# Opening a four-layer backbone by pairs of modulation units, moving one output tile behind the long convolution, and opening the windowed layer with two query tiles

## What is computed

```
m_lat = split(silu(c)     @ mod_w[i] + mod_b[i], 6)     # shift, scale, gate | shift, scale, gate
m_ctx = split(silu(c_ctx) @ mod_w[i] + mod_b[i], 6)
u     = rmsnorm(h, g[0]) * (1 + scale) + shift          # both streams
h     = h + gate * rmsnorm(mixer(u), g[1])
u     = rmsnorm(h, g[2]) * (1 + scale') + shift'
h     = h + gate' * rmsnorm((silu(dwconv(u @ w_gate)) * (u @ w_up)) @ w_down, g[3])
# A: q,k,v = u @ w_qkv; q,k normalised and rotated; softmax(q k) v @ w_out
# B: x0,x1,v = dwconv(u @ w_in); y = longconv(v*x1) + skip*v*x1; (y*x0) @ w_out + b_out
# C: as A with a bias on q,k,v and on the output, a window of +-128, a sink logit per head
```

## Time and profile before

| | us |
|---|---|
| median of 3 runs | 2288.19 |
| profiled execution, its own time | 2291.39 |
| its span | 2289.6 |
| TensorE (PE) busy | 2175.4 (95%) |
| VectorE (DVE) busy | 1437.8 (63%) |
| ScalarE (ACT) busy | 884.0 (39%) |
| a weight tile of 1 MB, from issue to landing (median) | 5.1 |

### The profile page before, as it was taken

How to read it: one execution, slowest core, us unless ns; L and a number is a source line. 1 busy time by engine, 2 the same in 40 slices (tenths; PEclk the granted TensorE clock), 3 DMA queues, 4 the chain that set the end, 5 groups by cost and what they waited for, 6 DMA issues and landing times.

```text
span 2289.6 us, 28755 instructions
## 1 busy us (share of the span) xinstructions
PE 2175.4 (95%) x11688; PEld 1767.1 (77%) x11688; DVE 1437.8 (63%) x2212; ACT 884.0 (39%) x1329; POOL 217.5 (9%) x253
## 2 busy tenths in 40 slices
PE   5999999999999988899999999999999999998998
PEld 3877888888787756788888787478888878868996
DVE  2426558887756532667887754866787776655553
ACT  3327443332244311443332243854333223455543
POOL 0000011110010014111110001100111100100110
PEclk7999999999999999999999999999999999999999
DMA  9460335546532210334546532022454563214554
GB/s 308 141 209 19 111 101 161 171 150 217 194 126 83 83 37 19 102 100 158 166 149 220 202 103 65 1 84 82 149 165 156 184 211 120 99 45 131 185 182 140
DMA packets 224745, 304.98 MB, mean 133 GB/s; under 512 B 6738, under 2 KB 153243, under 8 KB 224486
## 3 DMA queue, kind: packets, MB, share of 16 engines
q1 hardware_dynamic: 220541, 290.11, 39.0%
q0 software_dynamic: 3664, 12.87, 1.7%
q10 hardware_dynamic: 409, 0.16, 0.0%
HBM read 302.00 MB, written 1.11 MB: 132 GB/s over the span
## 4 chain that ended last, share of the span: by engine, by line
PE 78%; DVE 10%; ACT 5%; DMA 3%; issue 2%; SPq 1%; POOL 1%; ACTq 0%; DVEq 0%; POOLq 0%
PE lo L639 16%; PE lo L640 16%; PE lo L641 16%; PE lo L705 4%; PE lo L706 4%; PE lo L707 4%; DVE w_lo L1383 2%; ACT w_hi L1059 2%; PE lo L973 2%; PE hi L705 2%; PE hi L707 2%; PE hi L706 2%; DMA w_raw<-in_ffn_w_down 1%; PE hi L986 1%; PE stat L705 1%
## 5 line engine op out<-in xcount | busy, mean ns | idle before, releaser
L639 PE MATMUL lo<-u_hi,w_hi 128*128 128x512 f32 (+1 forms) x2072 | 736.5, 355 | 9.0 <-DVE w_lo L1383 3.8
L640 PE MATMUL lo<-u_lo,w_hi 128*128 128x512 f32 (+1 forms) x2072 | 723.2, 349 | 0.0
L641 PE MATMUL lo<-u_hi,w_lo 128*128 128x512 f32 (+1 forms) x2072 | 722.6, 349 | 0.0
L1383 DVE TENSOR_TENSOR w_lo<-w_raw,w_hi 128x2048 fp32r<-128x2048 f32 (+1 forms) x182 | 406.7, 2235 | 356.9 <-ACT w_hi L1059 355.7
L1059 ACT ACTIVATE w_hi<-w_raw 128x2048 fp32r<-128x2048 f32 (+1 forms) x182 | 339.5, 1867 | 478.9 <-DMA w_raw<-in_ffn_w_down 266.7
L639 PEld LDWEIGHTS lo<-u_hi,w_hi 128*128 128x128 f32 x2072 | 394.7, 191 | 74.1 <-issue 19.3
L641 PEld LDWEIGHTS lo<-u_hi,w_lo 128*128 128x128 f32 x2072 | 394.5, 190 | 50.1
L640 PEld LDWEIGHTS lo<-u_lo,w_hi 128*128 128x128 f32 x2072 | 394.7, 190 | 49.7 <-issue 1.2
L1400 DVE SCALAR_TENSOR_TENSOR mod_acc<-mod_raw,silu_c,mod_acc 128x512 f32<-128x512 f32 x504 | 394.6, 848 | 9.9 <-DMA mod_raw<-in_mod_w 9.9
L1912 POOL TENSOR_TENSOR mid_lo<-conv,mid_hi 128x512 fp32r<-128x512 f32 (+1 forms) x88 | 117.8, 1359 | 1055.7 <-ACT mid_hi L1362 1055.7
L705 PE MATMUL lo<-w_hi,mid_hi 128*128 128x512 f32 x374 | 147.4, 394 | 3.7 <-DVE u_raw L1450 2.6
(11 more groups left out here) (296 smaller groups left out, 2698.2 us busy)
## 6 DMA issues: line engine op xcount, KB each, us to landing
w_raw<-in_ffn_w_up SPq DMA_DIRECT2D x88, 1024.0 KB, 5.1
mod_raw<-in_mod_w SPq DMA_DIRECT2D x144, 512.0 KB, 4.0
w_raw<-in_ffn_w_down SPq DMA_DIRECT2D x40, 1024.0 KB, 5.1
mod_unit<-in_mod_w SPq DMA_DIRECT2D x24, 1024.0 KB, 6.8
w_raw<-in_a_w_qkv SPq DMA_DIRECT2D x12, 1024.0 KB, 5.2
w_raw<-in_b_w_in SPq DMA_DIRECT2D x12, 1024.0 KB, 5.1
w_raw<-in_a_w_out SPq DMA_DIRECT2D x8, 1024.0 KB, 5.1
w_raw<-in_ffn_w_down SPq DMA_DIRECT2D x8, 512.0 KB, 3.6
```

Of the source, the lines that this page charges most:

```text
L639: mm(o, h3[:, k, c], x, start=(first and k == 0), stop=False)
L640: mm(o, h3[:, k, c], y, start=False, stop=False)
L641: ins = mm(o, l3[:, k, c], x, start=False, stop=(last and k == nr - 1))
L1383: tt(WL[:, n % 3, 0:words], RAW[:, n % 3, 0:words], WH[:, n % 3, 0:words].bitcast(F32), ALU.subtract).then_inc(lo_ready, 1)
```

## The change

Four parts.

1. **Opening.** The units are loaded as shift 0, scale 0, shift 1, scale 1 and so on (`UNIT_COLS`), with weight tiles 0 and 1 after units 1 and 2, and tile 2 before the rope table and units 8 to 10. A pair p of units gives shift and scale of feature chunks 2p and 2p+1. After each pair VectorE finishes those (`start_mod`), TensorE turns both streams for them (`start_turns`), ScalarE and VectorE make `u_hi` and `u_lo` (`start_his`, `start_los`), and TensorE multiplies those two chunks for tiles 0 and 1 over all 512 tokens (`start_part`). `first_tiles` is not used for layer 0.
2. **Layer B.** `fill` is gone: the last inverse stands right behind the last forward and the third inverse, and output tile 0 comes after it, at the head of `x_phase`.
3. **Layer C.** The second tile is queries 1 instead of the key tile, which becomes the third; `CH`, `TURNS` and `TURN_AT` follow.
4. **End of every sub-layer.** A Sqrt of one element stands behind the squares of the first half, so the table for Sqrt is loaded there. In the output phases of B and C `lo(L+1)` moves from block 0 to block 1, behind the diagonal.

```
-        TILES += [("c_w_qkv", _j, 0, KT, 0, TW), ("c_w_qkv", _j, 0, KT, D, P)]
-        TILES += [("c_w_qkv", _j, 0, KT, TW * t, TW) for t in range(1, 4)]
+        TILES += [("c_w_qkv", _j, 0, KT, TW * t, TW) for t in range(2)]
+        TILES += [("c_w_qkv", _j, 0, KT, D, P)]
+        TILES += [("c_w_qkv", _j, 0, KT, TW * t, TW) for t in range(2, 4)]
...
-      2: [[0, 1], [8], [2, 3], [4, 5], [6, 7], [9]],
+      2: [[0, 1], [2, 3], [8], [4, 5], [6, 7], [9]],
...
+        UNIT_COLS = [0, 4, 1, 5, 2, 6, 3, 7] + list(range(8, MB))
...
             for r in range(8):
+                if r in (2, 3):
+                    raw(r - 2)
                 unit(r)
-                if r in (3, 5):
-                    raw(r // 2 - 1)
+            raw(2)
...
             pe.wait_ge(par_ready, 2)
-            u_turns(0, 0, range(KT))
             pe.wait_ge(silu_ready, 1)
-            for r in range(8):
+            def start_unit(r):
+                if r % 2 == 0 and r > 0:
+                    pe.wait_ge(mod_final, r // 2)
                 unit_rows(r)
+            def start_turns(p, v):
+                if p == 0:
+                    pe.wait_ge(diag_ready, 2 * v + 2)
+                if 2 * p + v >= 3:
+                    pe.wait_ge(u_ready, 2 * (2 * p + v - 2))
+                for c in (2 * p, 2 * p + 1):
+                    for e in range(2):
+                        ...
+                    last.then_inc(u_turned, 1)
+            def start_part(p, n):
+                if p == 0:
+                    pe.wait_ge(lo_ready, n + 1)
+                ...
+                for k in (2 * p, 2 * p + 1):
+                    if n == 0:
+                        pe.wait_ge(*u_part(0, 1, k))
+                    for m in range(2):
+                        ... (three matmuls of 512 tokens)
+            for r in range(2):
+                start_unit(r)
                 unit_cols()
+            start_turns(0, 0)
+            start_turns(0, 1)
+            start_unit(2)
+            start_part(0, 0)
+            unit_cols()
+            start_part(0, 1)
+            for v in range(2):
+                start_unit(3 + v)
+                start_turns(1, v)
+                unit_cols()
+            start_unit(5)
+            unit_cols()
+            start_part(1, 0)
+            start_part(1, 1)
+            for v in range(2):
+                start_unit(6 + v)
+                start_turns(2, v)
+                unit_cols()
+            start_turns(3, 0)
+            start_turns(3, 1)
+            for p in (2, 3):
+                start_part(p, 0)
+                start_part(p, 1)
...
                     if w < 3:
                         forward(w + 1)
-                    else:
-                        fill()
                     inverse(w)
...
+            unit_row(0)
+            unit_row(1)
+            hi(0)
+            start_his(0, 0)
+            start_his(0, 1)
+            hi(1)
+            unit_row(2)
+            unit_row(3)
+            unit_row(4)
+            start_his(1, 0)
+            start_his(1, 1)
+            unit_row(5)
+            unit_row(6)
+            start_his(2, 0)
+            unit_row(7)
+            start_his(2, 1)
+            start_his(3, 0)
+            start_his(3, 1)
...
                 for b in range(NB):
                     o_square(k, 0, b)
+                f(R1[:, 1, 4:5], eps[:, :], ACT.Sqrt)
...
-                    if b == 0:
+                    if b == 0 and not has_bias(k):
                         lo(L + 1)
...
                         diagonal(k + 1, b)
+                    if b == 1 and has_bias(k):
+                        lo(L + 1)
...
+            start_mod(0)
             lo(0)
+            start_los(0)
             lo(1)
-            finish_mod(0, 0)
-            u_los(0, 0)
-            u_los(0, 1)
+            for p in range(1, 4):
+                start_mod(p)
+                start_los(p)
```

More of the change, by code:

```diff
@@ L273, in build @@
                             ("x1v_tok", [P, 2, 2, 512], None), ("idft", [P, 4, SEQ], None))
-        MG = [place(f"mod_unit{s}", [P, KT, TW], at=U_AT + 8 * D * s) for s in range(4)]
+        MG = [None] * 4
         MG += region(*((f"mod_unit{s}", [P, KT, TW], 8 * D * (s - 4)) for s in range(4, 8)))
@@ L311, in build @@
         uh_ready, u_ready = sem("uh_ready"), sem("u_ready")
-        group_in = [sem(f"group_in{g}") for g in range(len(MG))]
+        group_in = [None] * 4 + [sem(f"group_in{g}") for g in range(4, len(MG))]
         group_done, group_rows, group_cols = sem("group_done"), sem("group_rows"), sem("group_cols")
@@ L695, in u_turns, with x_phase @@
                     last.then_inc(u_turned, 1)
-            def x_tiles(k, X, Y, arrive, free, ts, end=False):
+            def x_phase(k, X, Y, arrive, free):
                 n0, nt, NB = XFIRST[k], XTILES[k], XN[k]
@@ L719, in finished @@
                         ins.then_inc(x_done, 1)
-                for t in ts:
+                for t in range(2 * nt - 2):
                     n, (h, tt) = n0 + t, divmod(t, nt)
@@ L752, in x_tiles @@
                 n = n0 + 2 * nt - 2
-                for b in range(NB if end else 0):
+                for b in range(NB):
                     if nt == 2:
@@ new lines, in start_part @@
+            def start_part(p, n):
+                if p == 0:
+                    pe.wait_ge(lo_ready, n + 1)
+                h3, l3 = [W[:, n, :].rearrange("p (k n) -> p k n", n=TW) for W in (WH, WL)]
+                for k in (2 * p, 2 * p + 1):
+                    if n == 0:
+                        pe.wait_ge(*u_part(0, 1, k))
+                    for m in range(2):
+                        o, c = bank[2 * n + m], slice(m * P, (m + 1) * P)
+                        mm(o, h3[:, k, c], UH[:, k, :], start=(k == 0), stop=False)
+                        mm(o, h3[:, k, c], UL[:, k, :], start=False, stop=False)
+                        last = mm(o, l3[:, k, c], UH[:, k, :], start=False, stop=(k == KT - 1))
+                if p == 3:
+                    last.then_inc(tile_done, 1)
@@ L1037, in _ @@
                     free = lambda b, i=i: ((p_evac, ahead(NH, i) + NH[i]),) if b < 2 else ((ao_lo, ahead(GROUPS, i) + GROUPS[i] - 3 + b),)
-                x_tiles(2 * i, UH, UL, arrive, free, range(KIND[i] == 1, 2), end=True)
+                x_phase(2 * i, UH, UL, arrive, free)
                 n0, q0 = FIRST["up", i], PAIR0["up", i]
@@ L1159, in _, with start_his @@
                 h_root(0, b)
-            for r in range(8):
-                unit_row(r)
-                if r in (3, 5):
-                    hi(r // 2 - 1)
-            u_his(0, 0)
-            u_his(0, 1)
+            def start_his(p, v):
+                act.wait_ge(mod_final, p + 1)
+                act.wait_ge(u_turned, 4 * p + 2 * v + 2)
+                for c in (2 * p, 2 * p + 1):
+                    f(UH[:, c, v * SEQ:(v + 1) * SEQ], start_slot(p, v)[:, (c % 2) * SEQ:(c % 2 + 1) * SEQ], ACT.Identity,
+                      scale=coef[:, v, 0, c:c + 1], bias=modv[:, v, c:c + 1]).then_inc(uh_ready, 1)
+            unit_row(0)
[16 more added lines that the diff above has]
+            start_his(3, 1)
             def exps(i, x):
@@ L1400, in mod, with start_mod, start_los, difference @@
                             stt(acc, MR[:, k % 2, j, :], S2[:, s:s + 1], acc, ALU.mult, ALU.add).then_inc(mod_step, 1)
+            def start_mod(p):
+                dve.wait_ge(group_cols, 2 * p + 2)
+                c = slice(2 * p, 2 * p + 2)
+                for v in range(2):
+                    dst, src = [x.rearrange("p (j c) -> p j c", c=KT)[:, 0:2, c] for x in
+                                (modv[:, v, :], modp[:, v * NMOD * KT:(v + 1) * NMOD * KT])]
+                    ins = tt(dst, src, col("mod_b", 0, 2 * KT).rearrange("p (j c) -> p j c", c=KT)[:, :, c], ALU.add)
+                link(ins)
+                for v in range(2):
+                    ins = stt(coef[:, v, 0, c], modv[:, v, KT + 2 * p:KT + 2 * p + 2], 1.0, col("norm_g", 2 * p, 2), ALU.add, ALU.mult)
+                ins.then_inc(mod_final, 1)
+                dve.wait_ge(mod_final, p + 1)
+            def start_los(p):
+                def difference(v, c):
+                    dve.wait_ge(uh_ready, 4 * p + 2 * v + 2)
+                    s = slice(v * SEQ, (v + 1) * SEQ)
+                    stt(ULF[:, c, s], start_slot(p, v)[:, (c % 2) * SEQ:(c % 2 + 1) * SEQ], coef[:, v, 0, c:c + 1],
+                        UH[:, c, s].bitcast(F32), ALU.mult, ALU.subtract).then_inc(u_diff, 1)
+                parts = [(v, c) for v in range(2) for c in (2 * p, 2 * p + 1)]
+                difference(*parts[0])
+                for x, (v, c) in enumerate(parts):
+                    if x + 1 < 4:
+                        difference(*parts[x + 1])
+                    dve.wait_ge(u_diff, 4 * p + x + 1)
+                    s = slice(v * SEQ, (v + 1) * SEQ)
+                    ts(UL[:, c, s], ULF[:, c, s], modv[:, v, c:c + 1], None, ALU.add).then_inc(u_ready, 1)
```

(2 more changed lines are left out.)

52 lines of the change are left out of this document (30 added, 22 removed).

## The result

The changed kernel takes 2265.09 us (median of 4 runs, 2263.19 to 2271.05) beside 2289.24 for the kernel before (4 runs on the same chip, 2286.65 to 2291.05): ratio 0.990, 95% interval 0.9878 to 0.9921. That is 24.15 us less; 22.0 were predicted. The profiled execution took 2263.19 us, with a span of 2261.4.

The account below looks back on a forecast made before the run. It took TensorE's work to bound the kernel, with half clock and time without work to be saved. 12.3 + 6.5 + 6.0 + 0.5 - 3.3 = 22.0 us less, from 2288.19 to 2266.2; range for 8 in 10: 2258 to 2276.

Parts of the forecast that it names:

- Opening (-12.3): Opening, layer 0: tile 2 starts at 68.1 instead of 80.40 us, 12.3 us less; bounds 5 and 15.
- the 1.0 that I had added for a late rise of the clock: Opening: 1.0 us added to the worked 67.1 in case the clock rises later than 27 us.
- The claim that TensorE's own order sets the end: Opening: from 36 us on PE is behind the loads, so the order of its work sets the end.
- Rivals 1 and 4: Opening: half-clock stretch, gain 5 to 7 us, about 2272 (0.17); whole opening at half clock, slower than before, 2294.1 (0.03).
- Layer B (-6.5): Layer B's output: tile 1 no longer waits 6.26 us nor runs at half clock, 6.5 us less; bounds 5 and 7.
- Rival 3: Layer B gives nothing back, because tile 1 waits elsewhere, for bias or gates: 2273 us; chance 0.08.
- Layer C (-6.0): Layer C's projections: the 3.55 us wait and 2.7 of half clock go, 0.3 added: 6.0 less; bounds 3.3 and 6.3.
- Last A layer (-0.5): End of the last A layer's output: earlier table load takes 0.5 us off the 5.51 us wait.
- Ends of B's and C's output (+3.3): Turns at both outputs' ends: first wait shorter, second longer with clock lost, 3.3 us more in all; bounds 0 and 6.
- 1.35 us of clock: Ends of B's and C's output: net loss in each from half clock behind the longer second wait.
- the 0.3 us by which block 3 was to be later: Ends of B's and C's output: block 3's diagonal, which the context turns wait for, comes 0.3 us later.
- Rival 2: Ends of B's and C's output: longer second wait costs no clock, block 2 isn't late; 3 us better, 2263; chance 0.08.

Follow-up runs that it names:

- part 1 alone: Kernel before with only the new opening (load order of units, products of 512 tokens pair by pair): median 2274.51 us, against 2287.88 before.
- q_rows: Changed kernel with the eight row matmuls of units 3 to 7 done twice, more TensorE work in the opening: 2268.14 us in one run.
- part 3 alone: Kernel before with only queries 1 made layer C's second tile: median 2281.04 us, against 2287.88 before.
- part 4 alone: Kernel before with only the earlier Sqrt table load and lo(L+1) moved behind block 1's diagonal in B and C: 2288.12 us, against 2287.88 before.

## Why the prediction came out right, and where it didn't

- **Opening (-12.3).** Measured -13.03 in the trace (80.40 to 67.37), -12.45 in the trace of part 1 alone, -13.4 in its runs. The worked sum was 67.1; the 1.0 that I had added for a late rise of the clock wasn't needed, it rose by 26 us. Other traces of the same opening start tile 2 between 67.67 and 68.32 (69.32 where the clock fell at 43.9), so part of the 1.0 is the spread. The claim that TensorE's own order sets the end held (q_rows: 4.5 us for 4.3 of work). Rivals 1 and 4 are out.
- **Layer B (-6.5).** Arrival at the output's end went from 951.88 to 931.29, 20.59, of which 13.74 were gained by the last forward: -6.85. The new wait ahead of the last inverse was 1.84 (2.1 predicted), with no fall of the clock. Rival 3 is out.
- **Layer C (-6.0).** -18.0 at the head of the layer, -23.55 at its last projections: -5.5 in the trace, -6.8 in the runs of part 3 alone. What I missed is the 0.76 us that tile 1 waits for w_lo, now of a full tile. In the trace of the change the clock doesn't fall in C at all; with part 3 alone it fell behind C's first wait, at no cost.
- **Last A layer (-0.5).** 5.51 to 4.93: -0.58.
- **Ends of B's and C's output (+3.3): the step that failed.** It said that TensorE would wait above 4 us the second time and lose 1.35 us of clock at each place. The second wait was 2.6. In C TensorE gets there 0.4 us sooner after its arrival at the first turns and not 2 (17.05 us, 1547.19 to 1564.24, with part 4 alone; 17.43, 1547.47 to 1564.90, before), because inside the first turns it now waits 1.43 us for block 2's gate, late behind w_lo, to free a bank. I read who waits at the turns' head and not what their third and fourth quarters wait for.

  For B I had taken the second wait before to be as long as C's; it is 0.46. The clock was the other mis-sized term: the change lost none at its second waits, and in the five places of other traces where it did fall behind one, that cost 0.4 to 0.65 us and not 1.35 (last section). No wait above 4 us came there, so its price isn't shown. And the 0.3 us by which block 3 was to be later is 0.16. In C the place cost +0.16 instead of 1.65. Rival 2 (no clock lost, block 2 not late: 2263) is what C nearly shows; the median, 2265.09, lies between it and the forecast.

  In B the place cost 1.87, close to what I wrote for another reason: 0.17 from part 4 and 1.6 to 1.7 from the collision of two loads that part 2 brings together. For part 2 I had looked at what stands behind the last inverse on each engine, and not at whose load the later release of tile 0's buffer would meet.
- **Sum.** The places of the two profiles: -13.03 - 6.85 + 1.87 - 5.5 + 0.16 - 0.58 = -23.9, beside -24.15 in the medians. The profiles themselves differ by 28.2 (2291.39 to 2263.19). Of the other 4.3, 1.3 lie in layer C's attention and 1.6 in the last A layer's attention and output, where the clock fell in the trace of before (granted 0.50 from 1439.2 on and 0.51 from 2067.2 on, 3.4 us each) and not in that of the change; the last 1.3 are other waits in the last MLP. So that -23.9 comes so close to the medians is in part luck: each of the two traces is one execution of several.

The forecast was near for a mixed reason: the gains were to be 25.3 us and were 26.0, and a loss of 3.3 was 2.0, more than half of that 2.0 by a mechanism that I didn't have. That the loss came near its number is luck.

## What to carry to other kernels

When an instruction is moved off a wait, follow the same engine's next three waits, the ones inside a group of matmuls too: of C's first wait 2.05 us left (2.36 to 0.31), 1.43 came back inside the turns, and the second wait grew by 0.55 (2.08 to 2.63). When a buffer's release moves, look at which other queue loads at that time: 0.6 us in the order of two issues decided over 3 us of landing. And look for idle time on the chain's own engine (here 1.54 us a block, where half of w_lo takes 1.15) before moving work to another block.
